# A gated attention and mLSTM layer on one core: its front rebuilt around pairs of modulated feature tiles

## What is computed

```python
mod = silu(c) @ w_ada + b_ada;  shift, scale, gate = split(mod, 3)
h = rmsnorm(x, norm_w) * (1 + scale) + shift
aq, ak, av, az, mq, mk, mv, mo, mz, mi, mf, ga, gm = split(h @ w_in)
y_att = (window_attention(rope(aq), rope(ak), av, sinks) * silu(az)) @ w_att
hm    = mlstm(silu(conv(mq)), silu(conv(mk)) / 16, mv, mi + b_i, log_sigmoid(mf + b_f))
y_m   = (rmsnorm_per_head(hm) * m_norm_w * sigmoid(mo) * silu(mz)) @ w_m
merged = sigmoid(ga) * y_att + sigmoid(gm) * y_m
out = rmsnorm(x + gate * (merged @ w_out), final_norm_w)
```

## Time and profile before

| | |
|---|---|
| median of three runs | 1392.05 us |
| the profiled execution | 1391.64 us, of which the span 1389.9 us |
| busy PE, DVE, ACT, POOL | 1328.2, 668.1, 397.0, 662.6 us |
| PE starts its first matmul of h | 55.05 us after the span's start |
| the heads begin | 72.14 us |
| share of the chain that ended last | PE 82%, DVE 12%, ACT 2% |

### The profile page before, as it was taken

How to read it: one execution, slowest core, us unless ns; L and a number is a source line. 1 busy time by engine, 2 the same in 40 slices (tenths; PEclk the granted TensorE clock), 3 DMA queues, 4 the chain that set the end, 5 groups by cost and what they waited for, 6 DMA issues and landing times.

```text
span 1389.9 us, 20009 instructions
## 1 busy us (share of the span) xinstructions
PE 1328.2 (96%) x6846; PEld 1128.8 (81%) x6846; DVE 668.1 (48%) x1297; ACT 397.0 (29%) x926; POOL 662.6 (48%) x854
## 2 busy tenths in 40 slices
PE   3499999999999999999999999999999999999997
PEld 2398797989877888889978987898789888688886
DVE  5979886785873000153265235424542321544335
ACT  5334445353450100023322332333132311311111
POOL 6834507061366544295267146715661455557340
PEclk9799999999999999999999999999999999999999
DMA  9411102010021220230131031103210132321502
GB/s 350 123 45 31 47 2 61 15 32 28 0 61 61 75 79 26 89 93 17 48 89 30 0 90 46 30 0 92 59 30 15 45 92 91 106 91 61 197 16 106
DMA packets 119832, 89.30 MB, mean 64 GB/s; under 512 B 13305, under 2 KB 111721, under 8 KB 118894
## 3 DMA queue, kind: packets, MB, share of 16 engines
q1 hardware_dynamic: 116288, 76.16, 17.9%
q10 hardware_dynamic: 3502, 12.61, 2.6%
HBM read 80.35 MB, written 8.41 MB: 64 GB/s over the span
## 4 chain that ended last, share of the span: by engine, by line
PE 82%; DVE 12%; issue 2%; ACT 2%; DVEq 0%; ACTq 0%
PE pp L532 24%; PE pp L533 23%; PE pp L534 23%; PE pp L718 2%; PE pp L728 2%; PE pp L638 1%; DVE y_lo L1294 1%; DVE prob L1237 1%; DVE num L1404 1%; PE pp L710 1%; PE pp L621 1%; PE pp L629 1%; PE pp L723 1%; PE pp L622 1%; PE pp L607 1%
## 5 line engine op out<-in xcount | busy, mean ns | idle before, releaser
L484 POOL TENSOR_TENSOR w_hi<-raw,ones 128x256 fp32r<-128x256 f32 x404 | 284.1, 734 | 619.1 <-ACTq L346 341.0
L532 PE MATMUL pp<-h_hi,w_hi 128*128 128x512 f32 x912 | 361.5, 396 | 9.9 <-DVE h_lo L1120 8.3
L533 PE MATMUL pp<-h_lo,w_hi 128*128 128x512 f32 x912 | 356.1, 390 | 0.0
L534 PE MATMUL pp<-h_hi,w_lo 128*128 128x512 f32 x912 | 355.9, 390 | 0.0
L488 POOL TENSOR_TENSOR w_lo<-raw,w_hi 128x256 fp32r<-128x256 f32 x404 | 345.7, 887 | 7.9
L532 PEld LDWEIGHTS pp<-h_hi,w_hi 128*128 128x128 f32 x912 | 171.8, 188 | 49.6 <-issue 6.8
L534 PEld LDWEIGHTS pp<-h_hi,w_lo 128*128 128x128 f32 x912 | 171.8, 188 | 36.0
L533 PEld LDWEIGHTS pp<-h_lo,w_hi 128*128 128x128 f32 x912 | 171.9, 188 | 34.6
L532 PE MATMUL pp<-w_hi,h_hi 128*128 128x384 f32 (+1 forms) x512 | 162.1, 317 | 0.6 <-DVE roped L1214 0.6
L534 PE MATMUL pp<-w_hi,h_lo 128*128 128x384 f32 (+1 forms) x512 | 158.1, 309 | 0.0
L533 PE MATMUL pp<-w_lo,h_hi 128*128 128x384 f32 (+1 forms) x512 | 158.0, 309 | 0.0
(11 more groups left out here) (216 smaller groups left out, 1855.9 us busy)
## 6 DMA issues: line engine op xcount, KB each, us to landing
raw<-w_in SPq DMA_DIRECT2D x72, 512.0 KB, 3.6
w_mod<-w_ada SPq DMA_DIRECT2D x7, 1024.0 KB, 11.5
x_in<-x SPq DMA_DIRECT2D x4, 1024.0 KB, 8.0
raw<-w_att SPq DMA_DIRECT2D x8, 512.0 KB, 5.0
merged_dram<-mix_a ACTq DMA_DIRECT2D x8, 512.0 KB, 2.6
w_gate<-w_ada ACTq DMA_DIRECT2D x8, 512.0 KB, 3.4
raw<-w_m SPq DMA_DIRECT2D x8, 512.0 KB, 3.6
mix_in<-merged_dram ACTq DMA_DIRECT2D x8, 512.0 KB, 3.3
```

Source lines behind the costliest of these rows:

```text
L484: ins = pool.tensor_tensor(hi[:, q, :], raw[:, s, q, :], one[:, q, :], ALU.mult)
L532: pe.matmul(o, lh, rh, start=first, stop=False)
L533: pe.matmul(o, lh, rl, start=False, stop=False)
L534: return pe.matmul(o, ll, rh, start=False, stop=last)
```

## The change

- **Modulation in pairs.** w_ada is loaded by pairs of feature tiles: pair p is 256 columns of shift and 256 of scale, for all 1024 input features, two 1 MB transfers with 1 KB pieces. Of a pair's eight products, DVE makes the first 4, 6, 7 and 7 (512 columns each, the running sum in PSUM bank 6, the last into `mod_acc`), and PE makes the other 4, 2, 1 and 1 directly (`mod_part`) and sums DVE's across partitions with a column of ones (`mod_sums`). DVE adds both to `mod_b`.
- **x by token blocks.** DVE scales a block, PE turns its eight tiles into two banks, and DVE (six blocks) or ACT (two) writes it to `xnt` in one copy of 1024 columns.
- **Two last-gate tiles in the front.** Columns 0 to 255 of `gm` are loaded into slots 0 and 1. PE runs their four units tile by tile of h (12 matmuls each), in banks 2 to 5; ACT stores the sigmoids to DRAM (`early_dram`) and reads them back at D1. D1 keeps six tiles.
- **Gate columns on head 0.** `mi` and `mf` are 8 more columns of head 0's token units (392 instead of 384). They are turned once at the start of head 1, go through DRAM (`gate_dram`), and `gate_row_step` rides in head 1.
- **Splits.** h_lo of tiles 3 and 5 is made by POOL; ACT and DVE split slots 2 to 4 for head 0 and slot 1 of the early tiles. `raw`, `w_hi` and `w_lo` are laid out as [P, KT, 704].
- **Queues.** ACT issues the small vectors, SP positions, frequencies, pair 0, x, two `gm` tiles, pairs 1 to 3, the 8 gate columns. POOL makes the identity before it starts the counters.

```diff
+EARLY = 2
+J_PE = (4, 2, 1, 1)
+PART_BEFORE = {1: 1, 3: 2, 5: 3}
+SUMS_BEFORE = {2: 1, 3: 2, 5: 3}
+LO_BY_POOL = (3, 5)
-MOD_BY_ACT = (1, 4, 7)
+MOD_BY_ACT = (1, 3, 5, 7)
...
+            load_mod(0)
+            for n, blocks in enumerate(X_BLOCKS):
+                sp.dma_start(x_in[:, blocks, :], x_v[:, blocks, :]).then_inc(x_loaded[n], 16)
+            for n in range(EARLY):
+                sp.dma_start(raw[:, :, cols_of(n)], w_in_v[:, :, GM + n * P:GM + (n + 1) * P]).then_inc(slot_loaded[n], 16)
+            for p in range(1, PAIRS):
+                load_mod(p)
+            sp.dma_start(raw[:, :, GCOL:GCOL + G8], w_in_v[:, :, MI:MI + G8]).then_inc(g8_loaded, 16)
...
             for k in range(KT):
+                if k in PART_BEFORE:
+                    mod_part(PART_BEFORE[k])
+                if k in SUMS_BEFORE:
+                    mod_sums(SUMS_BEFORE[k])
...
+                for n in range(2 * EARLY):
+                    s, half = n // 2, n % 2
...
+                    ins = passes(bank(2 + n), (w_hi[:, k, cols_of(s)], w_lo[:, k, cols_of(s)]),
+                                 (h_hi[:, k, t], h_lo[:, k, t]), k, k == 0, k == KT - 1)
...
+                        dve.scalar_tensor_tensor(out=acc, in0=w_mod[:, :, p, j, :], scalar=silu_c[:, j:j + 1], in1=acc_ps,
+                                                 op0=ALU.mult, op1=ALU.add).then_inc(mod_summed, 1)
...
+            shift_scale(0)
+            split_h(0)
+            split_h(1)
+            mod_products(1, 0, KT)
+            mod_bias(1)
+            mod_products(2, 0, 2)
+            mod_scale(1)
+            shift_scale(2)
+            mod_products(2, 2, 3)
+            split_h(2)
+            mod_products(2, 3, KT)
+            mod_bias(2)
+            mod_products(3, 0, 2)
+            mod_scale(2)
+            shift_scale(4)
+            mod_products(3, 2, 3)
+            split_h(4)
+            mod_products(3, 3, KT)
+            mod_bias(3)
+            mod_scale(3)
+            shift_scale(6)
+            split_h(6)
+            split_h(7)
+            for s in range(2, 5):
+                after(dve, slot_hi[s], use("A", s, 1))
+                dve.tensor_tensor(w_lo[:, :, cols_of(s)], raw[:, :, cols_of(s)], w_hi[:, :, cols_of(s)].bitcast(F32),
+                                  ALU.subtract).then_inc(slot_split[s], 1)
...
-            for phase, hi, lo, ready in (("D1", h_hi, h_lo, None), ("D2", y2_hi, y_lo, y2_lo_ready)):
+            for e, (_, s, n) in enumerate(D1_TILES):
+                after(pe, slot_split[s], use("D1", s, n + 1))
+                for half in range(2):
+                    feature_unit("D1", 0, 0, 2 * e + half, s, half, h_hi, h_lo)
```

More of the change, by code:

```diff
@@ L361, in _ @@
         def _(sp):
[L362 to L367, removed]
@@ L375, in _ @@
[L375 to L380, removed]
+            sp.dma_start(pos_i[:, :], positions.rearrange("(n p) -> n p", p=P)).then_inc(pos_loaded, 16)
@@ L492, in loads @@
                 return before(SLOT_DMAS, phase, s) + n
-            split(4, use("G", 4, 0), loads("G", 4, 2))
-            with pool.Fori(0, KVH, 1) as i:
-                for s in range(5):
-                    per = 2 if s == 2 else 1
-                    split(s, use("A", s, 0) + i, loads("A", s, per) + per * i)
+            split(0, use("G", 0, 0), loads("G", 0, 1))
+            after(pool, slot_hi[1], use("G", 1, 1))
+            for q in range(4):
+                q = slice(2 * q, 2 * q + 2)
+                ins = pool.tensor_tensor(w_lo[:, q, cols_of(1)], raw[:, q, cols_of(1)], w_hi[:, q, cols_of(1)].bitcast(F32), ALU.subtract)
+            ins.then_inc(slot_split[1], 1)
+            for k in LO_BY_POOL:
+                pool.wait_ge(x_mod_act, sum(m in MOD_BY_ACT for m in range(k + 1)))
+                pool.wait_ge(h_hi_ready, k + 1)
+                for half in range(2):
+                    t = slice(half * HALF, (half + 1) * HALF)
+                    ins = pool.tensor_tensor(h_lo[:, k, t], x_mod[:, k, t], h_hi[:, k, t].bitcast(F32), ALU.subtract)
+                ins.then_inc(h_lo_late, 1)
+            for s in range(2):
+                split(s, use("A", s, 0), loads("A", s, 1))
+            with pool.Fori(0, KVH - 1, 1) as i:
+                for s in (2, 3, 4, 0, 1):
+                    per = 2 if s == 4 else 1
+                    split(s, use("A", s, 1) + i, loads("A", s, 2 * per) + per * i)
             for s in range(4):
@@ new lines, in mod_col, with mod_part @@
+            def mod_col(p, half, kk, summed):
+                c = 16 + 8 * p + 4 * summed + 2 * half + kk
+                return bank(7)[:, c:c + 1]
+            def mod_part(p):
+                pe.wait_ge(mod_loaded[p], 32)
+                if p == 0:
+                    pe.wait_ge(silu_c_ready, 1)
+                    pe.wait_ge(angle_step, 2)
+                else:
+                    pe.wait_ge(mod_step, 4 * p - 1)
+                for half in range(2):
+                    for kk in range(2):
+                        for j in range(KT - J_PE[p], KT):
+                            ins = pe.matmul(mod_col(p, half, kk, 0), w_mod[:, half, p, j, kk * P:(kk + 1) * P], silu_c[:, j:j + 1],
+                                            start=(j == KT - J_PE[p]), stop=(j == KT - 1))
+                ins.then_inc(mod_full, 1)
@@ new lines, in mod_sums @@
+            def mod_sums(p):
+                pe.wait_ge(mod_summed, sum(KT - J_PE[m] for m in range(p + 1)))
+                pe.wait_ge(mod_step, 4 * p + 1)
+                for half in range(2):
+                    for kk in range(2):
+                        ins = pe.matmul(mod_col(p, half, kk, 1), mod_acc[:, p % 2, half, kk * P:(kk + 1) * P], ones[:, 0:1],
+                                        start=True, stop=True)
+                ins.then_inc(mod_full, 1)
+            mod_part(0)
+            for n in range(NB):
+                if n == NB // 2:
+                    mod_sums(0)
+                pe.wait_ge(x_normed, n + 1)
+                if n >= 2:
+                    pe.wait_ge(x_evac, n - 1)
+                for k in range(KT):
+                    b = 2 + 2 * (n % 2) + k // 4
+                    ins = pe.transpose(bank(b)[:, k % 4 * P:(k % 4 + 1) * P], x_in[:, n, k * P:(k + 1) * P], ident[:, :])
+                ins.then_inc(x_turned, 1)
@@ L814, in _ @@
[L814 to L820 removed]
+            for n in range(X_BY_DVE, NB):
+                act.wait_ge(x_turned, n + 1)
+                act.activation(xnt[:, :, n * P:(n + 1) * P], x_block(n), ACT.Copy).then_inc(x_evac_act, 1)
```

525 lines of the change are left out of this document (310 added, 215 removed).

## The result

The changed kernel takes 1396.44 us (median of seven runs, 1394.55 to 1396.77), the one before 1392.05 (1391.73 to 1393.79, seven runs beside it). The ratio is 1.0027, with a 95% interval of 1.0018 to 1.0037: 4.4 us slower, where I had forecast 21.5 us faster. The profiled execution took 1395.34 us, its span 1393.6.

A forecast was written before the change was run, and what follows sets the result against it. It took VectorE's modulation chain to bound the front and TensorE's matmuls nearly all behind it. Span 1389.9 − 0.6 (front) − 20.7 (behind it) = 1368.6 us, with overheads 1370.5; 8-in-10 range 1360 to 1380.

The forecast's parts named there:

- Both signs: What would prove the forecast wrong: T outside 66 to 76, or stages behind the front besides D1 changing over 3 us.
- T: Time at which TensorE goes from the front to the heads: 72.14 us before, forecast 71.5.
- Rival 3: Front: strided loads at 130 GB/s run dry, T = 98, the kernel 1397 us; chance 0.04.
- What leaves D1: D1 loses two tiles, four feature units of 5.43 us each: 21.7 us saved on TensorE.
- Nothing replaces them as the bound of D1: D1: eight gate products in a row take 40 us, while six tiles still last 65 us.
- I take this as an exchange, zero: Heads 0 and 1: VectorE's gate-row work moves from head 0 to head 1 at no net cost, 2 us either way.
- The sum behind the front: All stages after the front: 21.7 − 0.7 − 0.3 = 20.7 us saved.
- x in place at 33 us: Front, step 1: x loaded, scaled, turned and copied by 33 us, with VectorE free for x near 15.5.
- VectorE's chain: Front, step 2: VectorE's remaining modulation, tile work and waits from 33 us to T, 39.0 us in sum.
- product pace: VectorE's 20 dependent modulation products of 512 columns in the front: 0.80 us each, 16.0 us in all.
- bias and scale of three pairs, nine tiny steps and their waits, 3.2 us: Front: VectorE's small modulation steps for pairs 1 to 3, including waits for TensorE, 3.2 us together.
- rival 2: Front: TensorE at 1.2 GHz paces the tiles, sums come late, T = 79.5, the kernel 1378.5 us; chance 0.16.

The follow-up runs named there:

- e6: Changed kernel with Exp and Ln of the gate rows in head 1 left out, two 8-column copies in their place: 1392.31 us.
- e3: Changed kernel with the gates turned and stored at the end of head 0, their bias, Exp and Ln at step 1 of head 1: 1397.51 us.
- e1: Changed kernel with the weight slots of B, C and D1 in the order in which they come free: 1384.07 us.
- e2: Changed kernel with only D1's slots in another order (2, 4, 0, 1, 2, 4): 1391.66 us.
- e4: Changed kernel with TensorE's modulation products and sums one tile earlier in its queue: 1390.62 us.
- e13: e10 with 8 more unread matmuls behind pair 1's one-column products: 1376.26 us.
- e10: Changed kernel with slots reordered, sums earlier, Exp and Ln late in head 1, plus 14 unread matmuls in TensorE's idle time before tile 0: 1377.81 us.
- e11: Changed kernel with slots reordered, sums earlier, Exp and Ln late, plus the gates' transpose behind head 0's last unit: 1378.01 us.

## Why the prediction was wrong

Both signs that I had named came: T at 79.5, outside 66 to 76, and stages behind the front that change by more than 3 us besides D1. Rival 3, the dry loads, gives 1397 us, next to the measured 1396.4; that is chance, for its T was 98, and neither TensorE nor VectorE waits for a transfer from 12 us to the heads.

1. **What leaves D1: right.** 21.7 us forecast, 22.3 measured. "Nothing replaces them as the bound of D1" held.
2. **"I take this as an exchange, zero": wrong by 6.7 us.** I compared the busy shares of two heads and gave the row work ±2 us. It is not its amount that counts but its place: in head 0 Exp and Ln ran before ScalarE had its first copy to make, in head 1 they stood between a rope and a softmax (e6: 5.7 us between heads 0 and 2). Head 0 gained 4.0 us and head 1 lost 11.6. I had looked for a round trip that makes ScalarE wait; that was hidden, until e3 exposed it.
3. **The starts of B and D2, at nothing and without a reason: wrong by 12.1 us.** "The sum behind the front" has no term for them; no step of mine looked at the order of slots. I had followed TensorE's and VectorE's queues, but not GpSimd's: the change gives the heads and D1 another last slot, and the next stage's splits begin with just these. e1 and e2 show it. This is the largest term, and no rival had it.
4. **x in place at 33 us: 36.8.** I had VectorE free for x at 15.5 us; it began at 19.76. Of these 4.3 us, 2.5 are the small vectors: VectorE starts its angle steps at 10.6 and not at 8. TensorE's four products of pair 0, which I had priced at nothing, make it wait another 1.9. Earlier vectors alone would not have helped much, for x too was late: its first load landed at 14.2, not 12, and its scale was ready at 17.7. A further 0.8 was lost in my own sum: 31.3, 1.3 and 1.2 are 33.8, and I wrote 33. The timelines of both engines show TensorE's part. Its products begin only when ScalarE has made silu(c), which comes behind VectorE's first four angle steps and its copy of the vectors (the row names the angle step beside it):

```profile
12.69 6.96 PE L631 MATMUL pp<-silu_c,w_mod 128*128 128x1 f32 x32 [3.55 <-DVE ang L1197]
19.68 0.16 DVE L1229 TENSOR_TENSOR mod_b<-pp,mod_b 128x4 f32<-128x4 f32 x1 [1.91 <-PE pp L631]
19.76 2.73 DVE L1261 TENSOR_SCALAR x_in<-x_in,x_rstd 128x1024 f32<-128x1024 f32 x4
```

   No experiment changed this; it is read from the trace.
5. **VectorE's chain.** The product pace was right (0.78 us a step against 0.80), `h_lo` a little shorter (1.28 against 1.43 in the mean). The term that failed is "bias and scale of three pairs, nine tiny steps and their waits, 3.2 us": the waits alone were 7.0. It is rival 2's mechanism in the main: products and sums that VectorE wants stand behind whole tiles in TensorE's queue, and tiles 0, 2 and 3 took 4.1 to 4.5 us each and not 2.9, at 0.43 us a matmul for half or more of them. But tile 1, which the rival has at half the clock, ran at 0.23. That its T of 79.5 was met to 0.1 us is chance: the tiles began 3.8 us later than it assumes, and fewer of them were slow. e4 took back 5.8 us by the order alone, e13 another 1.6 by the clock. What the clock alone would give in the changed kernel's order no run shows.

The rule of the Trainium skill that I weighed ("TensorE: Matmul & The Clock Gate", section "HAM oscillation — how this bites in real kernels") was right to speak against the change, and I gave its rival too small a chance, 0.16. Two of the four slow stretches above agree with it: they stand behind waits of 5.00 us (0.57) and 3.15 us (0.60). The other two (0.58 and 0.59) do not stand behind such a wait; TensorE had waited at most 0.35 us at a time since the tile ahead of them, and had run products and sums of one column. In e10 and e13 the clock is worth about 2 us (1.6 by the medians, 2.5 from the first tile to the heads), less than the order of the sums.

e13's 1376.26 us lies in the range, 5.8 above the value. It mends the starts of B and D2 and the order and clock of the front, but of heads 0 and 1 only 1.7 of the 7.5 us (171.1 us from head 0 to head 2), and x not at all. By the marks of the table its heads begin 2.8 us later than the 71.5 of the forecast (74.31), and the heads take 3.2 us more than forecast (341.3 us to B's first sigmoid, before 337.1, forecast 338.1). All the later stages are within 0.3 us of the forecast. Open is what the heads still lose, and a rest of up to 1.6 us between executions with the same heads (172.1 to 173.8 us from head 0 to head 2 in e4 and e1); I have no cause for it.

## What to carry to other kernels

When a change alters which buffer is released last, follow the fixed order of every engine that refills buffers in the stages behind it, not only in the stage changed: a refill that waits for the last buffer holds up those of buffers long free, and whatever else the engine owes. A short job moved to another place costs what is queued behind it there, not what it costs in busy time. Small products that another engine waits for belong ahead of the long ones in an in-order queue, and a wait that disappears is worth only what is not waited for under another name next (e10, e11).

## What the runs showed of the hardware

- TensorE's clock fell although TensorE was listed as fully busy. In the changed kernel it was busy 4.00 of 4 us from 60 to 64 us, at a clock of 0.58. Ahead of this stood products and sums of one column, from 58.0 to 60.2 us. TensorE's timeline shows these at the length that they have at the full clock (eight in 0.95 us; in e10, at half the clock, 1.22), and then the 512-column ones going from 0.48 to 0.63 us:

```profile
58.03 0.95 PE L631 MATMUL pp<-silu_c,w_mod 128*128 128x1 f32 x8
...
60.21 0.48 PE L581 MATMUL pp<-h_hi,w_hi 128*128 128x512 f32 x1
...
60.83 0.63 PE L583 MATMUL pp<-h_hi,w_lo 128*128 128x512 f32 x1
```

  The profile lists such matmuls as busy. That they let the clock fall is not shown: behind the 1.84 us of them at 44.9 us it stayed at 1.00 until 53 us, and in e13 it stayed at 1.00 through all of them, with 8 matmuls of 512 columns put only behind those of pair 1.
- Keeping one stretch warm moved the slow one behind the next wait (e10): the clock paid only when the whole chain of waits was covered.
- Transfers with 1 KB pieces ran at 380 to 384 GB/s (22 to 34 and 36 to 40 us), and at 312 where 512-byte pieces were mixed in (40 to 44 us); I had taken 350. From 12 us to the heads neither TensorE nor VectorE waited for one; ScalarE waited 1.6 us for the first load of x.
